# A hybrid RG-LRU, Fourier and attention backbone on one core: the rounds' modulation as VectorE sums instead of two-column matrix products

## The reference, cut to what matters

```python
def modulation(cvec, w_mod, b_mod):
    m = jax.nn.silu(cvec) @ w_mod + b_mod
    return jnp.split(m, 3, axis=-1)          # shift, scale, gate
...
for layer in range(DEPTH):
    sh_l, sc_l, gt_l = modulation(c, p["w_mod"], p["b_mod"])
    sh_c, sc_c, gt_c = modulation(c_ctx, p["w_mod"], p["b_mod"])
    h_lat = rms_norm(x, p["g_pre"]) * (1.0 + sc_l[:, None, :]) + sh_l[:, None, :]
    ...   # mixer: layer 0 is RG-LRU heads + 2-D Fourier mixing, layer 1 is windowed attention
    x = x + gt_l[:, None, :] * rms_norm(y_lat, p["g_post"])
```

## Time and profile before

| | us |
|---|---|
| median of 3 runs | 1620.65 (1617.24 to 1626.74) |
| profiled execution, its own time | 1625.64 |
| its span, first to last instruction | 1623.8 |

### The profile page before, as it was taken

The page is one execution under the profiler, slowest core; times in us unless marked ns, Lnnn a source line. Parts: engine busy times, 40 slices in busy tenths (PEclk is TensorE's granted clock), DMA queues, the critical chain, the costliest instruction groups (busy, mean ns, idle before and its releaser), DMA issues. The chain is left out here.

```text
span 1623.8 us, 21351 instructions
## 1 busy us (share of the span) xinstructions
PE 1489.6 (92%) x7894; PEld 1267.9 (78%) x7894; DVE 756.1 (47%) x1108; ACT 731.9 (45%) x1154; POOL 567.8 (35%) x267
## 2 busy tenths in 40 slices
PE   6989999999999999994899994999998799999697
PEld 6877888888888888883788883778886678887476
DVE  6345554546364645554211123412122688887632
ACT  4127372727273736353222222222222688888321
POOL 0003323132322222223434331524443466666332
PEclk9668999999999999997999997999999899999799
DMA  8111212121313030207443434444442733222584
GB/s 329 65 46 67 103 40 102 39 102 39 103 37 115 26 115 26 103 14 247 163 117 109 123 104 150 149 117 130 129 129 78 218 106 107 74 97 66 154 231 133
DMA packets 95432, 178.63 MB, mean 110 GB/s; under 512 B 10480, under 2 KB 57360, under 8 KB 93200
## 3 DMA queue, kind: packets, MB, share of 16 engines
q1 hardware_dynamic: 95376, 177.89, 34.3%
HBM read 122.79 MB, written 45.11 MB: 103 GB/s over the span
## 5 line engine op out<-in xcount | busy, mean ns | idle before, releaser
L684 PE MATMUL slab<-h_hi,w_hi 128*128 128x512 f32 x744 | 271.5, 365 | 1.5 <-DVE h_lo L518 1.5
L685 PE MATMUL slab<-h_lo,w_hi 128*128 128x512 f32 x744 | 269.4, 362 | 0.0
L686 PE MATMUL slab<-h_hi,w_lo 128*128 128x512 f32 x744 | 269.3, 362 | 0.0
L657 POOL TENSOR_TENSOR w_lo<-wraw,w_hi 128x1024 fp32r<-128x1024 f32 x32 | 80.0, 2501 | 478.4 <-ACT w_hi L391 478.4
L684 PEld LDWEIGHTS slab<-h_hi,w_hi 128*128 128x128 f32 x744 | 142.6, 192 | 25.1 <-DVE h_lo L518 1.6
L685 PEld LDWEIGHTS slab<-h_lo,w_hi 128*128 128x128 f32 x744 | 142.7, 192 | 23.4
L686 PEld LDWEIGHTS slab<-h_hi,w_lo 128*128 128x128 f32 x744 | 142.6, 192 | 23.4
L1659 POOL TENSOR_TENSOR probs<-probs,rdenom 128x2560 f32<-128x2560 f32 (+1 forms) x32 | 135.7, 4242 | 58.1 <-DVE rdenom L1619 58.1
L1374 PE MATMUL slab<-h_hi,w_hi 128*128 128x512 f32 (+1 forms) x352 | 135.3, 384 | 18.1 <-DVE h_lo L1296 17.7
L1104 PE MATMUL Y<-wo_hi,m_hi 128*128 128x512 f32 x320 | 127.4, 398 | 22.6 <-DVE wo_lo L1019 19.1
L1375 PE MATMUL slab<-h_lo,w_hi 128*128 128x512 f32 (+1 forms) x352 | 135.0, 384 | 0.0
(11 more groups left out here) (248 smaller groups left out, 3115.9 us busy)
## 6 DMA issues: line engine op xcount, KB each, us to landing
wraw<-in_w_in SPq DMA_DIRECT2D x32, 512.0 KB, 4.2
wm<-in_wm SPq DMA_DIRECT2D x32, 512.0 KB, 3.4
mixT<-work SPq DMA_DIRECT2D x16, 640.0 KB, 5.3
mraw<-mixT SPq DMA_DIRECT2D x20, 512.0 KB, 5.2
wm<-in_wm SPq DMA_DIRECT2D x8, 1024.0 KB, 17.5
q_parts<-qT SPq DMA_DIRECT2D x32, 256.0 KB, 4.6
oT<-o_out SPq DMA_DIRECT2D x8, 1024.0 KB, 3.9
x_tiles<-in_x SPq DMA_DIRECT2D x10, 512.0 KB, 7.9
```

The lines of the kernel that those rows point to most:

```text
L684: nc.tensor.matmul(out, l_hi, r_hi, start=start, stop=False)
L685: nc.tensor.matmul(out, l_hi, r_lo, start=False, stop=False)
L686: return nc.tensor.matmul(out, l_lo, r_hi, start=False, stop=stop)
```

## The change

The host lays the weights out with the output channel on the partition and all 1024 input channels on the free axis, and hands over the two conditioning vectors as rows (`c_rows`). Before the rounds, SP broadcasts these rows to all partitions, ACT takes the tanh and DVE makes twice the silu of them. In the rounds DVE multiplies the 128 x 1024 weights of one q by the silu row of one vector and sums along the free axis into one column; it does so for both vectors (w), so two instructions per q, eight per round. PE's modulation products go. `load_mod` now waits for both sums of the q before. To make room, `y_hi` and `y_lo` share the memory of `pq_hi` and `pq_lo`, and ACT's wait for the output products moves from the copy into `pq_hi` to the copy into `y_hi`.

```diff
-        y_hi, y_lo = sb("y_hi", [P, T], F32R), sb("y_lo", [P, T], F32R)
+        y_hi, y_lo = pq_hi[:, 0:T], pq_lo[:, 0:T]
-        wm1 = sb("wm1", [P, KT, P])
+        wm1 = sb("wm1", [P, D])
+        silu_b, th_b = sb("silu_bcast", [P, 2, D]), E[:, 0:D]
+        m_out = sb("mod_terms", [P, D])
...
             def load_mod(t, q, first):     # SP
-                    sp.wait_ge(mp, N_MOD * t + q)
+                    sp.wait_ge(mp, 2 * (N_MOD * t + q))
...
+            sp.dma_start(silu_b[:], a["c_rows"].partition_broadcast(P)).then_inc(cb_ld, 16)   # SP, before the rounds
...
             # ACT, round body
                 act.wait_ge(yr, t + 1)
                 if not first:
-                    act.wait_ge(dft, t)
-                nc.scalar.activation(y_hi[:], xf[:], ACT.Copy).then_inc(yh, 1)
+                    act.wait_ge(uv, t)
+                nc.scalar.activation(y_hi, xf[:], ACT.Copy).then_inc(yh, 1)
...
                 act.wait_ge(dft, t + 1)
-                if not first:
-                    act.wait_ge(uv, t)
...
             # ACT, after the tables, before the rounds
+            act.wait_ge(cb_ld, 16)
+            for w in range(2):
+                if w:
+                    act.wait_ge(sbd, 1)
+                nc.scalar.activation(th_b, silu_b[:, w, :], ACT.Tanh, scale=0.5).then_inc(thb, 1)
...
             # DVE, after its memsets, before the rounds
+            for w in range(2):
+                dve.wait_ge(thb, w + 1)
+                nc.vector.scalar_tensor_tensor(out=silu_b[:, w, :], in0=th_b, scalar=1.0, in1=silu_b[:, w, :],
+                                               op0=ALU.add, op1=ALU.mult).then_inc(sbd, 1)
+            dve.wait_ge(sbd, 2)
+
+            def mod_sums(t, q):
+                dve.wait_ge(m_ld, 16 * (N_MOD * t + q + 1))
+                for w in range(2):
+                    if not (isinstance(t, int) and t == 0 and q == 0 and w == 0):
+                        dve.wait_ge(mp, 2 * (N_MOD * t + q) + w)
+                    nc.vector.scalar_tensor_tensor(out=m_out[:], in0=wm1[:], scalar=0.5, in1=silu_b[:, w, :],
+                                                   op0=ALU.mult, op1=ALU.mult,
+                                                   accum_out=m_acc[:, q, w:w + 1]).then_inc(mp, 1)
...
                 nc.vector.tensor_scalar(cur[:], cols[:, :, t], 1.0, None, ALU.mult).then_inc(cu_, 1)
+                mod_sums(t, 0)
...
+                mod_sums(t, 1)
                 direction(0)
+                mod_sums(t, 2)
                 scan(0)
...
                 direction(1)
+                mod_sums(t, 3)
                 dve.wait_ge(pqh, t + 1)
...
             # PE: mod_product and its four calls go
-                for k in range(KT):
-                    last = nc.tensor.matmul(m_cols[:, q, :], wm1[:, k, :], silu_c[:, k, :],
-                                            start=(k == 0), stop=(k == KT - 1))
-                last.then_inc(mp, 1)
...
         # host
-        "wm1": np.concatenate([wm0[:, :, 2:], wm1], 2).transpose(3, 2, 1, 0, 4),
+        "wm1": np.concatenate([wm0[:, :, 2:], wm1], 2).transpose(3, 2, 4, 0, 1).reshape(KT, N_MOD, P, D),
+        "c_rows": np.stack([g["c"][0], g["c_ctx"]]),
```

More of the change, by code:

```diff
@@ L273, in mixers @@
         E = sb("E", [P, CONV_N])
-        y_hi, y_lo = sb("y_hi", [P, T], F32R), sb("y_lo", [P, T], F32R)
         pq_hi, pq_lo = sb("pq_hi", [P, PQ_N], F32R), sb("pq_lo", [P, PQ_N], F32R)
+        y_hi, y_lo = pq_hi[:, 0:T], pq_lo[:, 0:T]
         wf = sb("wf", [P, P])
         ab_hi, ab_lo = sb("ab_hi", [P, 2 * P], F32R), sb("ab_lo", [P, 2 * P], F32R)
-        wm1 = sb("wm1", [P, KT, P])
-        m_sum = sb("mod_sum", [P, N_MOD, 2])
+        wm1 = sb("wm1", [P, D])
+        silu_b, th_b = sb("silu_bcast", [P, 2, D]), E[:, 0:D]
+        m_out = sb("mod_terms", [P, D])
+        m_acc, m_sum = sb("mod_acc", [P, N_MOD, 2]), sb("mod_sum", [P, N_MOD, 2])
         g_rows = E[0:2 * KT, 0:2 * P].rearrange("p (i n) -> p i n", n=P)
-        m_cols = W4[:, 256:256 + 2 * N_MOD].rearrange("p (q w) -> p q w", w=2)
         Wf = W[:].rearrange("p b n -> p (b n)")
@@ L307, in mixers @@
         m_ld, mp, mb, me = sem("wmod_loaded"), sem("mod_product"), sem("mod_biased"), sem("mod_columns_done")
+        cb_ld, thb, sbd = sem("cond_rows_loaded"), sem("tanh_rows"), sem("silu_rows")
         gt_, ge, gst = sem("gates_transposed"), sem("gate_rows_copied"), sem("gate_rows_stored")
@@ L637, in body @@
                 stt(out=H[:], in0=H[:], scalar=0.5, in1=B[:], op0=ALU.mult, op1=ALU.mult).then_inc(mr, 1)
-                dve.wait_ge(mp, N_MOD * t + N_MOD)
-                tt(m_sum[:], m_cols, cur[:, C_MODB:C_MODB + N_MOD].unsqueeze(2).to_broadcast([P, N_MOD, 2]),
+                dve.wait_ge(mp, 2 * (N_MOD * t + N_MOD))
+                tt(m_sum[:], m_acc[:], cur[:, C_MODB:C_MODB + N_MOD].unsqueeze(2).to_broadcast([P, N_MOD, 2]),
                    ALU.add).then_inc(mb, 1)
@@ L669, in body @@
                 pool.wait_ge(yh, t + 1)
-                sub(y_lo[:], xf[:], v32(y_hi[:]), ALU.subtract).then_inc(yl, 1)
+                sub(y_lo, xf[:], v32(y_hi), ALU.subtract).then_inc(yl, 1)
                 if not last:
@@ L771, in body @@
                     first_products()
-                    mod_product(t, 0, first)
                 else:
                     slab_product(t, SLAB_U, first)
-                    mod_product(t, 0, first)
                     slab_product(t, SLAB_F, first)
-                mod_product(t, 1, first)
                 pe.wait_ge(fr, 3 * t + 3)
@@ L798, in body @@
                 slab_product(t, SLAB_GF, first)
-                mod_product(t, 2, first)
                 gate_products(t, 1)
@@ L812, in body @@
                 last.then_inc(uv, 1)
-                mod_product(t, 3, first)
             set_tensor(pe)
```

## The result

| | us |
|---|---|
| kernel before, median of 7 runs | 1620.65 (1616.86 to 1630.61) |
| kernel after, median of 7 runs | 1632.49 (1628.56 to 1633.97) |
| ratio | 1.0059, 95% interval 1.0031 to 1.0088 |

The new kernel is about 0.6% slower. The forecast was 1624.2, in a range of 1588 to 1648: a change of 3.5 us, where the medians differ by 11.8. The profiled execution took 1631.20, 5.6 more than the profiled one before (1625.64); its span is 1629.4. TensorE's busy time fell by 34.5 us (1489.6 to 1455.1) and VectorE's rose by 98.6.

What follows compares the result with a forecast made beforehand. PE was taken to bound the rounds. Six middle rounds -8.1, round 0 +4.5, last +0.35 and clock +6.8 gave +3.5 us: 1624.2 against the median 1620.65, with a range of 1588 to 1648.

Steps and rivals of the forecast that it cites:

- waits before the transposes and before the DFT take the place of the products: PE in a round: 0.64 us wait before the transposes, DFT 0.35 later; removing q 0 to q 2 gains nothing.
- the term's price: Each accumulating VectorE instruction over 128x1024 was put at 1.28 us, 2.56 a q.
- Rival B: VectorE's accumulating form runs at the scan's rate, 2.35 us a term; 1653 to 1666 us in all; chance 0.11.
- the taking of turns at q 2: Before scan(0), q 2's terms and GpSimd's w_lo and y_lo run in series; scan(0) ends at 309.5.
- Rival A: Terms overlap with GpSimd or y_lo slips behind; DFT 4.3 us earlier than walked; 1583, up to 1605; chance 0.22.
- q 0, q 3, and the shared y at nothing: q 0 and q 3 fit VectorE's idle time; ScalarE's moved wait for the output products is long over: no cost.
- the gate reads: ScalarE's six reads between scan(0) and the DFT take 3.51 us, so the DFT starts at 313.2.
- the clock: PE's longer waits before the DFT let its clock fall to 1.2 GHz, 1.7 us a fall, 6.8 in all.
- I take one in every other round, 0.85 x 8 = 6.8: Clock falls at PE's waits: ends were none and two a round; one in every other round assumed, 6.8 us.
- rival C: TensorE's clock falls at both waits of each round, before the fifth gate product and the DFT; 1645 us; chance 0.11.
- Round 0: Silu rows delay the taps; transposes 4.45 us later, q 3's removal saves 1.70; +4.5 in all, bounds +2 to +9.

Runs made afterwards that it cites:

- GpSimd short: New kernel with GpSimd's w_lo of slab G and y_lo cut to one column in rounds 1 to 7; 1582.50 us, 0.9762 of the kernel before.
- q 0 and q 3 twice: New kernel with each term of q 0 and q 3 computed a second time into another accumulator; 1632.73 us, 1.0053 of the kernel before.
- shared y: Kernel before with only y's memory shared with pq and ScalarE's wait moved; 1626.42 us, ratio 1.0017.
- both moved: New kernel with q 1's sums moved behind the convolution and q 2's behind the silu of gf; 1590.33 us, 0.9806 of the kernel before.
- PE filled: New kernel with 26 unused matmuls on PE ahead of the fifth gate product; 1611.63 us, 0.9948 of the kernel before.
- q 2 late: New kernel with only q 2's sums moved, behind the silu of gf; 1599.55 us, 0.9867 of the kernel before.
- q 1 early: New kernel with only q 1's sums moved, ahead of the butterfly; 1601.05 us, 0.9873 of the kernel before.
- rows early: "both moved" with the silu rows made inside the set-up's loop; 1579.92 us, 0.9747 of the kernel before.
- bank waits: "rows early" with the DFT waiting for the gate reads one bank at a time; 1576.27 us, 0.9700 of the kernel before.

## Why the prediction held, and which of its terms were off

**Right: waits before the transposes and before the DFT take the place of the products.** Counted by starts, as the forecast did, the transposes come 0.63 after the F slab (288.00 - 287.37), where 0.64 was walked; the idle column, 0.47, leaves out what the last matmul needs to drain. From the fifth gate product's turn (309.58) to the DFT are 6.06 us where the kernel before took 2.01: 4.05. The DFT itself takes 2.21 more. 0.63 + 4.05 + 2.21 = 6.9: there are the 6.8 us that left the queue.

**Right: the term's price.** 1.28 a term was forecast; start to start it is 1.26 (295.15 to 296.41), of it 1.225 the operation and 0.081 the readout, partly overlapped. Rival B (2.35) is refuted. So is here what the Trainium skill states in "Vector Engine (DVE) Microarchitecture Reference", section "Points that are easy to get wrong", a halved rate for two SBUF sources that aren't bf16: both sources are float32 in SBUF, an accumulator is written, and the 1024 elements take the 1.225 us that they took without one.

**Right: the taking of turns at q 2**, with each end within half a microsecond. The walk had `scan(0)` end at 309.5; it ended at 312.32 - 3.24 = 309.1. Rival A (overlap) is refuted by the stretched rows, and "GpSimd short" shows its time: with the stretch away, a round is 6 us shorter, the clock's 2.2 included, and the kernel takes 1582.5, where A had put 1583. As walked, the load of q 2 was not last: it had landed by 301.25, before w_lo ended at 302.70.

**Right: q 0, q 3, and the shared y at nothing**, by "q 0 and q 3 twice" and "shared y". After q 3, pq_lo waits 1.14 for ScalarE and the scan's product 1.51, as in the earlier trace rows.

**Off by 0.8 us a round, too pessimistic: the gate reads.** ScalarE's six reads were put at 3.51, their length in the earlier trace rows. There they followed PE one by one. Now four of the six products were long ready, and the six reads took 3.15 (the same in "both moved"); with the 0.4 of the scan the DFT started at 315.64 - 3.24 = 312.4 and not 313.2. This made the chain's part of a middle round about -2.2 us, not -1.35.

**Off by 1.35 us a round, too optimistic: the clock.** The step that failed in size is "I take one in every other round, 0.85 x 8 = 6.8". The fall came in every round and cost some 2.2, by "PE filled" and by the DFT's own length. Over the eight DFTs it is 17.4 us instead of 6.8 (46.6 against 8 x 3.65), and alone it would have brought the forecast to 1635. That rival C's two falls a round did not come is seen in the same place: PE's wait before the DFT is only 0.67, and both waits are followed by one stretch at 0.50.

The two errors nearly cancel in the rounds, and that is luck. A round was forecast at -0.5, with the clock, and came at -0.16 (78.60 to 78.44), a mean over seven.

**Round 0: nearly right, by errors that cancel too.** The ruler row of round 0 does not yet show the 1.70 of its q 3, which PE saves ahead of the next slab. So at that row the forecast is 4.5 + 1.70 + 0.85 = 7.05 later, and measured from the last `h_lo` of the set-up it is 7.3 (73.24 before, 80.55 after). Its parts: the transposes came 3.9 later, where 4.45 was forecast; from the transposes to the DFT are 0.87 more (28.24 against 27.37) and not 3.09 - 1.28 = 1.81; and the DFT took 6.16 for 3.66, so the clock cost 2.50 there and not 0.85.

**The rest of the miss.** Between the two profiled executions the forecast was +3.5 (1625.64 to 1629.1), and +5.6 was measured: round 0 +7.3, seven rounds -1.0, set-up -2.3 (its last `h_lo` at 109.79 before, 107.52 after), behind the rounds +1.6. The last two have no cause in the change that any run shows: over all kernels here, none of which changes anything behind the rounds, that stretch lies between 888.9 and 892.7. So of the 8.3 us between forecast and median only 2.1 lie between the two profiled executions. Another 5.0 come from stepping down from the profiled execution to the median before, and 1.3 from the new kernel's median above its own profiled execution.

The chances, last: 0.35 stood on "within 0.5%", 0.38 on slower. The measured 0.59% is just over that border, and its interval crosses it. Had the fall of the clock been put in each round, as the longest wait the chain made was the same in each round, the sum would have said 1635 and "slower".

## What to carry to other kernels

Work taken off the busiest engine is worth what the next chain leaves of it; put the new work where its engine idles and its neighbour with the shared access is quiet, not where the program text happens to have a natural place. On TensorE count a wait together with what the clock does to the work behind it: here a wait of 3.44 us cost some 2.2 more in every pass of the loop, and filling it gave all of that back. Shortening it to 1.3 gave it back in most passes and not in all, so a time read from one pass of such a loop can mislead: look at every pass.

## What the runs showed of the hardware, not expected

**The two engines take turns operation by operation.** When VectorE and GpSimd both have operations with two SBUF inputs queued, neither keeps the access: it goes to and fro after each, and both rows show a stretched duration, which is waiting and not work. VectorE's term shows 3.87 for 1.22, GpSimd's w_lo 3.49 for 2.42. VectorE's pq_lo, which reads one input from PSUM, was not stretched: 2.02 beside GpSimd's w_lo, before and after.

**The longer the wait, the more often TensorE's clock fell, but its length alone does not decide.** Counted are the waits before the fifth gate product and, 2 us of work later, before the DFT; a DFT of 4.96 us or more is one at the lower level.

| first wait, second wait (us) | where | at the lower level |
|---|---|---|
| 3.27 to 3.46, 0.56 to 0.88 | new kernel, "q 0, q 3 twice", rounds 1 to 7 | 14 of 14 |
| 2.17 to 2.53, 1.14 | new kernel, "q 0, q 3 twice", "GpSimd short", round 0 | 3 of 3 |
| 1.11 to 1.33, 1.11 to 1.15 | "q 2 late", rounds 1 to 7; "q 1 early", all | 6 of 15 |
| at most 0.46, 0.79 to 1.15 | "both moved", "PE filled", "rows early", rest of "GpSimd short", round 0 of "q 2 late" | 0 of 32 |

In rounds 1 to 6 of "q 1 early" the two waits are alike to 0.03 us, and three of the six fell. A wait of 3.08 in the kernel before was not followed by a fall, one of 2.89 was the earlier trace rows. And in the set-up of the kernel before the clock is at the lower level right behind 4.84 us of two-column matmuls, with no wait at all: the rows of 512 columns then take 0.63 instead of 0.40.

```profile
91.23 4.84 PE L250 MATMUL W<-silu_c,wm 128*128 128x2 f32 x32
...
96.50 0.63 PE L685 MATMUL slab<-h_lo,w_hi 128*128 128x512 f32 x1
```

What decides in these cases was not tried and stays open.

**The set-up runs at a different clock from one execution to the next.** Between 30 and 100 us PE is granted 0.68 in the kernel before and 0.79 in "shared y", whose code is the same there, and the set-up's last `h_lo` starts at 109.8 and 99.8. In "rows early", where it is all but the same, they are 0.81 and 99.0. The kernels "PE filled" and "GpSimd short" also had the early one (101.6, 102.1), "q 2 late" and "bank waits" the late one (109.7, 109.8). Columns as in the earlier trace rows, before, "shared y" and "rows early":

```profile
30.00:100.00 70.00, 68.53 (x359) 62.75 (x358) 25.95 (x42) 13.08 (x15) 2.42 (x1) 0.68 0.19 72
```

```profile
30.00:100.00 70.00, 69.70 (x409) 64.01 (x410) 28.68 (x47) 16.32 (x19) 2.42 (x1) 0.79 0.23 81
```

```profile
30.00:100.00 70.00, 68.67 (x413) 62.64 (x413) 31.85 (x50) 20.13 (x22) 2.44 (x1) 0.81 0.26 96
```

That is some 10 us in 1620 with no cause in the change, as large as the difference between some of these kernels. It is why rounds were compared by the ruler row inside one trace and not by medians alone. What decides between the two was not tried.
